# Hybrid decoder layer on one core: GpSimd issues the merge of the first six tiles behind the loads of the late tiles' sums

## The reference

```
xn     = RMSNorm(x1)
routed = sum over a token's 8 chosen experts of weight * SwiGLU(xn; w_gate[e], w_up[e], w_down[e])   # 64 experts
out    = x1 + routed + SwiGLU(xn; w_sh_gate, w_sh_up, w_sh_down)                                     # the shared expert
```

## Time and profile before

| What | us |
|---|---|
| median of three runs | 1524.55 |
| profiled execution, its time | 1521.13 |
| its span, first to last instruction | 1519.4 |
| TensorE busy | 1480.7 (97% of the span) |
| VectorE, ScalarE, GpSimd busy | 664.3, 299.3, 678.9 |
| granted TensorE clock, mean over the span | 0.99 |

### The profile page before, as it was taken

The page is one execution under the profiler, slowest core; times in us unless marked ns, Lnnn a source line. Parts: engine busy times, 40 slices in busy tenths (PEclk is TensorE's granted clock), DMA queues, the critical chain, the costliest instruction groups (busy, mean ns, idle before and its releaser), DMA issues.

```text
span 1519.4 us, 24188 instructions
## 1 busy us (share of the span) xinstructions
PE 1480.7 (97%) x6703; PEld 660.1 (43%) x6704; DVE 664.3 (44%) x887; ACT 299.3 (20%) x567; POOL 678.9 (45%) x638
## 2 busy tenths in 40 slices
PE   7999999999999989999999999999999999999994
PEld 3556556556556433333333333333333333333332
DVE  2444354453452534444444444444444444444441
ACT  1223323323332201111111111111111111111110
POOL 2010212222131524566556655665566556665661
PEclk9999999999998999999999999999999999999998
DMA  9411211211162449989898988888899898898927
GB/s 347 156 51 51 77 42 36 77 42 35 64 277 112 176 153 318 323 264 315 284 341 271 323 273 269 253 259 257 266 345 345 282 319 267 291 307 251 330 38 175
DMA packets 74572, 328.96 MB, mean 217 GB/s; under 512 B 15162, under 2 KB 16699, under 8 KB 48807
## 3 DMA queue, kind: packets, MB, share of 16 engines
q1 hardware_dynamic: 44438, 248.04, 44.0%
q0 software_dynamic: 30096, 80.45, 22.2%
HBM read 284.31 MB, written 65.11 MB: 230 GB/s over the span
## 4 chain that ended last, share of the span: by engine, by line
PE 92%; DMA 2%; DVE 2%; issue 2%; POOL 1%; ACT 1%; another core or an unknown queue 0%; SPq 0%; POOLq 0%; DVEq 0%; ACTq 0%
PE psP L697 53%; PE psW L697 30%; PE psT L850 5%; PE psW L912 1%; DMA area<-x_dram 1%; PE psW L748 1%; DMA wts<-in_w_in_dram 1%; POOL slot_table L593 0%; PE psT L705 0%; PE psT L784 0%; PE psT L770 0%; DMA slot_table<-pay,slot_i 0%; ACT area L1079 0%; PE psW L725 0%; POOL x_dram L657 0%
## 5 line engine op out<-in xcount | busy, mean ns | idle before, releaser
L697 PE MATMUL psP<-wts,bias 128*64 (+1 forms) x1296 | 574.2, 595 | 1.3 <-DVE bias L1527 1.3
L697 PE MATMUL psP<-area,bias 128*64 128x512 f32 x1264 | 559.4, 595 | 0.0
L697 PE MATMUL psW<-wts,area 128*64 (+2 forms) x1592 | 428.2, 594 | 3.3 <-DVE area L1687 1.3
L697 PEld LDWEIGHTS psP<-wts,bias 128*64 128x64 f32 (+1 forms) x1296 | 172.4, 138 | 336.1 <-issue 336.1
L657 POOL DMA_INDIRECT out_dram<-area,sidx x79 | 172.5, 2183 | 278.2 <-ACT area L1189 203.3
L697 PE MATMUL psP<-wts,area 128*128 128x512 f32 (+1 forms) x704 | 289.0, 562 | 5.7 <-DMA wts<-in_w_in_dram 4.4
L657 POOL DMA_INDIRECT x_dram<-area,sidx x79 | 252.8, 3201 | 24.4 <-issue 24.4
L697 PEld LDWEIGHTS psW<-wts,area 128*64 128x64 f32 (+1 forms) x1592 | 150.5, 148 | 253.9 <-issue 247.8
L1569 DVE COPY wts<-wts 128x2048 f32 x79 | 96.9, 1227 | 298.3 <-issue 298.3
L1561 DVE COPY area<-wts 128x4096 f32 x81 | 186.0, 2296 | 24.9 <-issue 20.4
L697 PEld LDWEIGHTS psP<-wts,area 128*128 128x128 f32 x704 | 132.2, 193 | 137.5 <-issue 128.5
(11 more groups left out here) (215 smaller groups left out, 826.9 us busy)
## 6 DMA issues: line engine op xcount, KB each, us to landing
wts<-in_w_exp_gate_dram SPq DMA_DIRECT2D x64, 1024.0 KB
wts<-in_w_exp_up_dram SPq DMA_DIRECT2D x64, 1024.0 KB
wts<-in_w_exp_down_dram SPq DMA_DIRECT2D x64, 1024.0 KB, 7.1
wts<-in_w_in_dram SPq DMA_DIRECT2D x4, 2048.0 KB, 17.6
area<-in_x_dram SPq DMA_DIRECT2D x8, 512.0 KB, 3.5
wts<-in_w_out_dram SPq DMA_DIRECT2D x1, 4096.0 KB, 18.3
area<-u_dram SPq DMA_DIRECT2D x16, 256.0 KB, 2.8
xn_dram<-area POOLq DMA_DIRECT2D x8, 512.0 KB
```

Of the source, the lines that this page charges most:

```text
L697: return nc.tensor.matmul(out_, lhsT, rhs, start=start, stop=stop)
```

## The change

GpSimd gets two waits ahead of the merge: it now waits until the loads of both late tiles have landed. Nothing else differs.

```diff
@@ -684,6 +684,8 @@
             for b in range(2):
                 pool.wait_ge(s_added[b], n * 16)
             carry(pool)
+            for t in range(NLATE):
+                pool.wait_ge(ab_ld[t], 32)
             rows = 2 * P
             for a in range(NSH * P // rows):
                 pool.dma_start(out2[a * rows:(a + 1) * rows, :].rearrange("(p r) n -> p (r n)", r=2),
```

## The result

The changed kernel took 1531.97 us in the median of 20 runs (1524.16 to 1537.43), the kernel before 1526.64 us in the median of 20 (1520.76 to 1531.41). The ratio is 1.003 with a 95% interval of 1.0017 to 1.0042, a loss of 2.6 to 6.4 us. The forecast was a loss too small for a single comparison of this kernel, 1.7 us, a time of 1525.5 us in a range of 1519.5 to 1532.0. The loss is 5.3 us by the medians, three times the forecast one; in the end of the program, where the change acts, it is 3.76 us in the trace, about twice.

The account below looks back on a forecast made before the run. The sum of DMA work, not one transfer, was taken to bound the end. The merge would land last at 1516.9 against 1515.2 us, 1.7 us slower; added to two bases (1526.3, 1524.5), 1525.5 us was taken, range 1519.5 to 1532.

Parts of the forecast that it names:

- loads landed: Late tiles' loads, running alone at 391 GB/s: last byte at 1496.3 us, landed 1497.2 us.
- merge issued: GpSimd starts 0.6 us after what it waits for: merge issued at 1497.8 us, 7.8 us later than before.
- first store beside nothing, in the hole: First late tile's store, issued at 1497.33 us as before, takes 1.35 us in the gap before the merge.
- merge's first packets: Queue q0: first bytes 1.2 us after the merge's issue, at 1499.0 us; upper end 4 us, at 1501.8.
- merge's engine time: Merge's 3.14 MB: 15.6 us of all 16 DMA engines, 202 GB/s, as beside the other queue before.
- One of the signs named: Second late tile's store beside the merge: needs up to 6.8 us; both stores landed before 1511 us.
- A: Merge after 1499.0 us: alone it runs at the plain rate, 8.1 us; 5.8 us less, 1519.7 us; chance 0.08.
- B: Merge after 1499.0 us: without other packets it runs at 132 GB/s, 23.8 us; 9.9 us more; chance 0.08.
- C: End of program: store covers the hole, merge wins back a microsecond; 0 to -1 us, 1524 us; chance 0.18.
- the base: End of program: loss counted from the last store's landing at 1515.2 us, keeping 4.2 us to the span's end.
- The bound of 4.5 us above: Hole before the merge: loss at most 4.5 us, 1.7 plus 2.8 more to the first bytes.
- The rule weighed in the prediction: Merge's transfer: about 2.0 us plus bytes at 436 GB/s, an estimated 9.2 us instead of 15.6, a gain.

Follow-up runs that it names:

- the second trace: The changed kernel run again, unaltered, against the kernel before: tail (last scatter's issue to end of span) 36.07 us, ratio 1.0022 (1.0007 to 1.0038).
- the merge alone: Against the changed kernel, GpSimd's merge waits until both late tiles' stores have landed: tail 41.43 us, ratio 1.0071 to the kernel before.
- the small DMA: Against the kernel without the merge, GpSimd issues one plain 4 KB DMA after both stores have landed: tail 25.23 us, one run.

## Why the prediction was right in its sign and half the size

Against its own steps, in + times:

| Step | forecast | measured |
|---|---|---|
| loads landed | +10.35 | +10.9 |
| merge issued | +10.95 | +11.47 |
| first store beside nothing, in the hole | yes | yes, 1502 to 1503.3 us |
| merge's first packets | 1.2 us after its issue | 1.6 to 1.8 us after |
| merge's engine time | 15.6 us | 16.2 us, 15.8 in the second trace |
| last merge landed | +30.05 | +31.2 |
| second store issued | 7.9 us earlier in its span | +15.6 instead of +23.5, 7.9 earlier |
| second store landed | by about +24 | +26.4 |
| from the last landing to the end | 4.2 us, behind a store | 5.1 us, behind the merge |
| the loss | 1.7 us | 3.76 us |

**The mechanism held.** The merge starts behind the loads, a hole opens in the DMA share, and the merge becomes the last to land. No byte and no engine time was saved. One of the signs named failed, without harm: the second store needed 10.8 us beside the merge and not at most 6.8, and landed at +26.4, still ahead of the merge. The rivals A and B fall with the merge alone. C, nothing moves, falls with the tails: 36.31 and 36.07 us against 32.55 and 32.23.

**The first term mis-sized is the base.** The prediction measured the loss from the last store's landing at 1515.2 us and kept the 4.2 us from there to the end of the span. The store had no part in it. The merge had landed at 1514.2 us and GpSimd's drain was what ran until 1519.1. So the merge's delay had to be counted from 1514.2, 1.0 us more, the largest single error. The tail of the changed kernel ends 5.1 us behind the merge's landing, where the sum had 4.2 behind the last one.

**The second is the merge's start**, 1.15 us in all: the merge was issued 0.5 us later than forecast because the loads landed 0.55 us later, its first packets came 0.5 us later after that, and from there to the last landing it took 18.1 us instead of 17.9, at first with only 137 GB/s (1504 to 1507 us). 1.7 + 1.0 + 1.15 = 3.85, against 3.76 measured.

The bound of 4.5 us above held in the tail. The median lies at 1531.97, 5.3 us above that of before, 1.6 more than the tail explains. The interval of the ratio (2.6 to 6.4 us) holds 3.76, and the second measurement gave 3.3 us (1.1 to 5.8), so I leave the rest to the scatter, which is not shown.

The predicted time was 6.5 us low, by two errors of the same sign: 3.6 us are the loss, and 2.8 us the base, since 20 runs of the kernel before gave 1526.64 and not the 1523.8 that stood under the forecast. That the measured time still fell inside the range, at its very edge, is **luck** and no merit of the sum: the upper end had been set by the slowest of four executions. The lower end was also reasoned wrongly. Rival A's 1519.7 takes its 5.8 us off the forecast, which already holds the loss; off the median of 1524.55 it is 1518.7, under the range that was said to hold it.

The rule weighed in the prediction, of the Trainium skill, DMA: Bandwidth & Descriptors, section Anatomy of one DMA — SWDGE (gpsimd) path, about 2.0 us plus the bytes at 436 GB/s, comes near the small DMA (an estimated 2.0 us, landed after 1.7) and not the merge (17.7 us alone, from issue to landing, where the rule would make an estimated 9.2).

## What to carry to other kernels

At the end of a program don't ask only which transfer lands last, but on which engine's end the program waits: read each engine's last instructions. A DMA issued by GpSimd had 4.9 us of drain behind it here, one by SP 0.2 to 0.4, so GpSimd's go first and SP's into the drain's shadow, even if the last byte then lands later. And where the DMA engines are full, holding one transfer back for another moves work but removes none (the merge took 15.2 to 16.2 us of the engines in every order tried). Here it paid where it let GpSimd's last DMA land earlier, and it cost where it opened a hole ahead of that DMA.

## What the runs showed of the hardware

- GpSimd's drain at the program's end is over 4.8 to 5.0 us after the last DMA that it issued has landed, for three merges of 1 MB and for one copy of 4 KB alike. With its last DMA already landed when it began, it took 5.7 us.
- An accumulating DMA between two places in device memory ran at 216 GB/s by itself, about half the 389 to 418 GB/s of plain loads and stores on the same engines. Whether the add or the two ends in device memory halve the rate, no run here tells.
- Where the merge was issued beside the loads of the other queue, its first packets came 3.7 to 4.4 us after its issue, in six traces (before: the earlier trace rows). Where it was issued when the loads were through or within 2 us of it, they came 1.6 to 1.8 us after, in five; those of the 4 KB copy came 1.2 us after.
